# A two-block transformer on one core: the order of steps in the second attention

## The chip, the cores and the metric

The kernel runs on one NeuronCore of a Trainium2 chip. The core has five engines with a queue of instructions each: TensorE (matrix products and transposes, called PE in the profile; its loads of stationary operands are PEld), VectorE (DVE), ScalarE (ACT), GpSimd (POOL) and SyncE (SP), which here issues the transfers. The metric is the device time of one execution in microseconds.

## What is computed

Two transformer blocks on 512 positions of width 1024, in float32. The change touches one part of the second block, the latent attention of its second layer:

```python
def latent_attention(h, pos, w_in, q_norm, kv_norm, w_uq, w_ukv, q_gain, k_gain, w_out):
    c = h @ w_in
    c_q, c_kv, k_rope = jnp.split(c, [Q_LORA, Q_LORA + KV_LORA], axis=-1)      # 256, 128, 32
    q = (rmsnorm_2(c_q, q_norm) @ w_uq).reshape(B, S, B_HEADS, dqk)            # 16 heads, 96
    kv = (rmsnorm_2(c_kv, kv_norm) @ w_ukv).reshape(B, S, B_HEADS, QK_NOPE + V_DIM)
    k_nope, v = jnp.split(kv, [QK_NOPE], axis=-1)                              # 64, 64
    k = jnp.concatenate([k_nope, broadcast k_rope], axis=-1)
    q = rmsnorm_2(q, q_gain); k = rmsnorm_2(k, k_gain)
    # rotary embedding of the last 32 of the 96, causal softmax over 512 keys, then
    # o = p @ v for each head, and o @ w_out
```

Before and behind it stand feed-forward layers (width 2816, three products each), which take most of the time.

## The kernel before

Everything stays on the chip; weights stream in once, as tiles. Products are done in float32 accuracy by splitting each operand in a high part (rounded, written by ScalarE) and a low part (the rest, written by VectorE or GpSimd) and adding three products (lines 1058 to 1060): low by high, high by low, high by high. So nearly every operand costs one ScalarE and one VectorE instruction.

The program is one list of steps, made by `order` and, for this attention, by `attend_b_order`. Each engine walks the same list in order and emits its own part of each step; within an engine nothing is reordered. What links them are semaphores: a step waits for named events of other engines. The order in which steps are listed is therefore the order of work on every engine at once. Buffers go round in rings (`Ring`): `take` gives the next slot and makes its new user wait until the last one has freed it. `banks` are the eight PSUM banks, `tmps` three slots of TMP; `part(k)` cuts a ring off.

The attention runs so. Latents (`b_latent`): c_q in two products (0, 1), c_kv in one (2), k_rope in `b_kr`; ScalarE copies and squares, `b_sumsq` adds the squares with matmuls of one column (line 1295), and `b_factors` turns the sums into the latents' norms on VectorE (lines 2125 to 2145, with a root by three Newton steps). Then the heads come in groups g of two: four units (`b_unit`), u = 2, 3 for keys and values, u = 0, 1 for queries. ScalarE squares a unit (lines 1615, 1623) into the tmps slot and copies it (1619, 1627, 1634), VectorE adds the squares (2154) and makes the values' low part (2162). GpSimd rotates the queries (`b_rotate`, 2298 to 2304), norms both (`b_norm`, 2313 to 2319, the third a power) and scales the keys (`b_scale`, 2329 and 2333).

The head loop then has a software pipeline in it: pass i does the scores of head i (`b_scores`: products at 1333 to 1335, on VectorE the masked maximum at 2186), its exponentials (`b_exp`, 1653), the turning of the next head's queries and keys (`b_qk`: 1069, 1643, 2169), the sum and scaling on GpSimd (`b_sum`: 2200, 2340), the turning of head i - 2 (`b_turns`, three parts of 4, 4 and 2 transposes, line 1343; `b_pt_hi`, 1662; `b_pt_lo`, 2194), and the product with the values of head i - 3 (`b_values`). Passes 0 to 11 also do two units of group i // 2 + 2, and passes from 11 on a part of the output product. Rings in the loop: three banks for scores, two for turned parts, one for the values' sums and two for all else (turned queries and keys, units, output). Two of the three tmps slots are held for exponentials (`third`). ScalarE's split of the weight tiles (1395) and GpSimd's low part (2237) run between these steps.

Of the kernel before, what the change touches and what calls it, by code (L numbers as in the profile page):

```python
# [11 lines left out]
ALU = mybir.AluOpType  # L12
# [4 lines left out]
EPS = 1e-6  # L17
# [720 lines left out]
def attend_b_order(banks, tmps, next_tile, norm_step, hkeys, h_new, h_pair, stats, add_x, do):  # L738
    do("b_begin")

    def latent(i, n):
        banks.take(("b_c", i))
        tmps.take(("t_bc", i))
        do("b_latent", i, n, hkeys())
        norm_step()
# [7 lines left out]
    banks.take(("b_ss",))  # L753
    do("b_sumsq", 1)
    n = next_tile("bq", 0)
# [3 lines left out]
    latent(1, n)  # L759
    do("used", n)  # L760
    do("b_sumsq", 0)
    do("b_factors")

    third = tmps.part(2)
    for n in (3, 2):
        third.take(("t_e", n))
    scored, turned, summed = banks.part(3), banks.part(2), banks.part(1)
    tile = {}

    def unit(g, u):  # L770
        if (u, g % 2) == (2, 0):
            tile[g // 2] = next_tile("bg", g // 2, 1)
# [9 lines left out]
    def head_qk(h):  # L782
        for name in ("b_qt", "b_kt"):
            banks.take((name, h))
        do("b_qk", h)
# [17 lines left out]
    for g in range(2):  # L803
        for u in (2, 3, 0, 1):
            unit(g, u)
        rotate(g)
        do("b_norm", g)
        do("b_scale", g)
    head_qk(0)
    LT, LV, LO = 2, 3, 11  # L810
    for i in range(16 + LV):
        t = i - LT
# [6 lines left out]
        if i < 16:  # L819
            for part in range(3):  # L820
                scored.take(("b_s", i, part))
                do("b_scores", i, part)
            do("b_exp", i, 0)
            if i < 15:
                head_qk(i + 1)
        if i >= LV:
            v = i - LV
            if v % 2 == 0:
                summed.take(("b_o", v // 2))
            do("b_values", v)  # L830
        if i < 16:
            do("b_exp", i, 1)
        if 0 <= t < 16:
            do("b_pt_lo", t, 0)
            do("b_pt_lo", t, 1)
        if i < 16:
            do("b_sum", i)
# [4 lines left out]
        if 0 <= t < 16:  # L842
            turned.take(("b_t", t, 2))
            do("b_turns", t, 2)
            do("b_pt_hi", t, 2)
            do("b_pt_lo", t, 2)
        if i >= LV and (i - LV) % 2:
            attended((i - LV) // 2)
        if i < 12 and i % 2:
            rotate(g)  # L850
            do("b_norm", g)
# [19 lines left out]
def build(nc, a, out, ctx):  # L871
# [182 lines left out]
    def pe_program(pe):  # L1054
# [26 lines left out]
        for kind, *s in steps:  # L1081
# [205 lines left out]
            elif kind == "b_sumsq":  # L1287
                e, = s
                o = vacant(("b_ss",))
# [3 lines left out]
                for n in range(4):  # L1293
                    for i in rows:
                        ins = mm(o[:, 4 * e + n:4 * e + n + 1], tmp(("t_bc", i))[:, 128 * n:128 * n + 128], ones[:, 0:1],
# [20 lines left out]
            elif kind == "b_qk":  # L1316
                h, = s
                x, hl = (h // 2) % 2, h % 2
                pe.wait_ge(*at(("b_rot", h // 2)))
                o = vacant(("b_qt", h))  # L1320
                four(o, lambda n: qts[x][:, n, hl, :], 96).then_inc(*bank_full.up(("b_qt", h)))
                pe.wait_ge(*at(("b_ks", h // 2)))
                o = vacant(("b_kt", h))
                four(o, lambda n: kts[x][:, n, hl, :], 96).then_inc(*bank_full.up(("b_kt", h)))
# [49 lines left out]
    def act_program(act):  # L1374
# [11 lines left out]
        for kind, *s in steps:  # L1386
# [210 lines left out]
            elif kind == "b_kr":  # L1597
                t = vacant(("t_kr",))
                act.wait_ge(*at(("b_kr",)))
                run(t[0:32, :], bank(("b_kr",))[0:32, :], ACT.Copy).then_inc(*act_out.up("b_kr_raw", free=("b_kr",)))  # L1600
            elif kind == "b_kr_turn":
# [5 lines left out]
            elif kind == "b_unit":  # L1607
# [13 lines left out]
                else:  # L1621
# [6 lines left out]
                    act.wait_ge(*at("b_lat"))  # L1628
# [7 lines left out]
            elif kind == "b_qk":  # L1636
                h, = s
                for e, (name, g) in enumerate((("b_qt", gq_b), ("b_kt", gk_b))):
                    act.wait_ge(*at((name, h)))
                    act.wait_ge(*at("small"))  # L1640
                    if h > 1:
                        act.wait_ge(*at(("b_s", h - 2, 2)))
                    run(QK[h % 2][e][0][0:96, :], bank((name, h))[0:96, :], ACT.Copy, scale=g[0:96, :]).then_inc(
# [835 lines left out]
```

## Time and profile before

| | |
|---|---|
| median of 3 runs | 2815.04 us (2812.4 to 2815.44) |
| profiled execution | 2825.3 us, its span 2824.1 us |
| TensorE busy | 2717.6 us, 96% of the span |
| VectorE, ScalarE, GpSimd busy | 1470.3, 974.7, 313.2 us |
| mean granted TensorE clock | 0.976 |
| the second attention, from its latents to its last head | about 2199 to 2429 us of the span |

The span goes from the first to the last instruction. Times in rows are microseconds from its start, unless marked ns. A row of a timeline gives start, duration, engine, line and operation, and in brackets how long the engine had been idle before and what released it. Matmuls overlap, so the sum of their durations is more than the time that they take. Granted clock 1.00 is 2.4 GHz, 0.50 is 1.2 GHz.

### The profile page before, as it was taken

The numbers are of one execution on the slowest core, as the hardware profiler recorded it, in microseconds if no ns is written. First come the engines' busy times: TensorE is split into PE (matmuls) and PEld (weight loads), VectorE is DVE, ScalarE is ACT, GpSimd is POOL, SyncE is SP. The second block draws the span as 40 slices with busy tenths as digits, with TensorE's granted clock in tenths as the row PEclk, the third lists the DMA queues.
The fourth block names the chain that finished last, engine by engine and source line by source line (L and its number), as shares of the span: only waits on it lengthen the run. The fifth ranks groups of instructions, "written<-read, shape, count | busy, mean of one in ns | idle before, by whom it ended". The sixth has DMA issues, their size and how long they took to land.

```text
span 2824.1 us, 32255 instructions
## 1 busy us (share of the span) xinstructions
PE 2717.6 (96%) x13207; PEld 2278.7 (81%) x13207; DVE 1470.3 (52%) x2347; ACT 974.7 (35%) x1601; POOL 313.2 (11%) x381
## 2 busy tenths in 40 slices
PE   6899999999998999998999999999999888999999
PEld 5788788888786888888878888888888778888887
DVE  4635546665657545556665343544434466544433
ACT  3334333333353212234453222322223466432221
POOL 2000000000021000003340000000000467400000
PEclk9999999999999999998999999999999889999999
DMA  4322233623132287746223333232322100132331
GB/s 137 103 92 75 75 105 128 196 79 109 55 115 75 90 104 90 105 84 120 76 65 105 105 98 96 90 105 91 98 94 84 38 31 31 60 119 90 95 96 64
DMA packets 281195, 258.99 MB, mean 92 GB/s; under 512 B 40517, under 2 KB 276056, under 8 KB 281048
## 3 DMA queue, kind: packets, MB, share of 16 engines
q1 hardware_dynamic: 281047, 256.93, 33.1%
q8 instruction: 104, 1.70, 0.3%
q14 instruction: 44, 0.35, 0.0%
HBM read 242.23 MB, written 14.68 MB: 91 GB/s over the span
## 4 chain that ended last, share of the span: by engine, by line
PE 84%; DVE 9%; ACT 4%; issue 1%; SPq 1%; POOL 1%; DMA 1%; DVEq 0%; ACTq 0%; POOLq 0%
PE bank L1058 27%; PE bank L1059 26%; PE bank L1060 26%; DVE Wl L1730 1%; PE bank L1201 1%; PE bank L1069 1%; ACT Wh L1395 1%; SPq L2421 1%; PE bank L1343 1%; DVE Pl L1718 1%; DVE TMP L1923 1%; DVE TMP L1920 1%; DVE TMP L1799 0%; ACT TMP L1508 0%; DMA RAW<-in_a_w_in 0%
## 5 line engine op out<-in xcount | busy, mean ns | idle before, releaser
L1058 PE MATMUL bank<-Hh,Wl 128*128 128x512 f32 x2144 | 845.9, 395 | 15.1 <-DVE Hl L1746 15.1
L1059 PE MATMUL bank<-Hl,Wh 128*128 128x512 f32 x2144 | 838.7, 391 | 0.0
L1060 PE MATMUL bank<-Hh,Wh 128*128 128x512 f32 x2144 | 838.5, 391 | 0.0
L1395 ACT ACTIVATE Wh<-RAW 128x1024 fp32r<-128x1024 f32 (+2 forms) x454 | 441.0, 1023 | 440.6 <-PE bank L1060 378.3
L1730 DVE TENSOR_TENSOR Wl<-RAW,Wh 128x1024 fp32r<-128x1024 f32 (+2 forms) x420 | 492.7, 1216 | 172.2 <-ACT Wh L1395 171.7
L1058 PEld LDWEIGHTS bank<-Hh,Wl 128*128 128x128 f32 x2144 | 404.7, 189 | 103.9 <-issue 8.2
L1058 PE MATMUL bank<-Ph,Wl 128*128 128x512 f32 x1200 | 474.5, 395 | 13.2 <-DVE Pl L1812 3.5
L1060 PEld LDWEIGHTS bank<-Hh,Wh 128*128 128x128 f32 x2144 | 404.5, 189 | 86.3
L1059 PEld LDWEIGHTS bank<-Hl,Wh 128*128 128x128 f32 x2144 | 404.7, 189 | 84.9 <-issue 1.7
L1059 PE MATMUL bank<-Pl,Wh 128*128 128x512 f32 x1200 | 470.6, 392 | 0.0
L1060 PE MATMUL bank<-Ph,Wh 128*128 128x512 f32 x1200 | 470.4, 392 | 0.0
L1788 DVE TENSOR_TENSOR bank<-bank,M 128x512 f32<-128x512 f32 x220 | 150.4, 696 | 387.1 <-PE bank L1060 382.3
L2244 POOL TENSOR_TENSOR TMP<-TMP 128x512 f32<-128x512 f32 x63 | 85.4, 1356 | 1932.1 <-ACT TMP L1417 1930.6
L1058 PEld LDWEIGHTS bank<-Ph,Wl 128*128 128x128 f32 x1200 | 227.4, 190 | 63.8 <-DVE Pl L1718 4.4
L1060 PEld LDWEIGHTS bank<-Ph,Wh 128*128 128x128 f32 x1200 | 227.4, 190 | 48.4
L1936 DVE SCALAR_TENSOR_TENSOR X<-bank,X 128x512 f32<-128x512 f32 x176 | 120.5, 689 | 278.0 <-PE bank L1060 277.4
L1059 PEld LDWEIGHTS bank<-Pl,Wh 128*128 128x128 f32 x1200 | 227.6, 190 | 46.6 <-issue 0.2
L1457 ACT ACTIVATE Ph<-TMP 128x512 fp32r<-128x512 f32 x110 | 69.6, 632 | 485.4 <-DVE TMP L1915 425.3
L1504 ACT ACTIVATE TMP<-bank 128x512 f32<-128x512 f32 x88 | 52.6, 599 | 258.8 <-DVE bank L1788 258.8
L1718 DVE TENSOR_TENSOR Pl<-TMP,Ph 128x512 fp32r<-128x512 f32 x126 | 87.3, 693 | 88.0 <-ACT Ph L1457 76.9
L1058 PE MATMUL bank<-Wh,Hl 128*128 128x256 f32 x288 | 85.5, 297 | 3.0 <-ACT M L1560 3.0
L1059 PE MATMUL bank<-Wl,Hh 128*128 128x256 f32 x288 | 84.1, 292 | 0.0
(296 smaller groups left out, 2506.4 us busy)
## 6 DMA issues: line engine op xcount, KB each, us to landing
RAW<-in_ffn_wg SPq DMA_DIRECT2D x44, 1024.0 KB, 5.3
RAW<-in_ffn_wu SPq DMA_DIRECT2D x44, 1024.0 KB, 5.3
RAW<-in_ffn_wd SPq DMA_DIRECT2D x32, 1024.0 KB, 5.2
RAW<-in_w_up SPq DMA_DIRECT2D x22, 1024.0 KB, 5.1
RAW<-in_w_in SPq DMA_DIRECT2D x20, 1024.0 KB, 5.1
RAW<-in_ffn_wd SPq DMA_DIRECT2D x16, 768.0 KB, 4.4
bias_scratch<-M SPq DMA_DIRECT2D x16, 512.0 KB, 8.0
RAW<-in_w_down SPq DMA_DIRECT2D x8, 1024.0 KB, 5.9
```

Source lines behind the costliest of these rows:

```text
L1058: mm(o, ll, rh, start=start, stop=False)
L1059: mm(o, lh, rl, start=False, stop=False)
L1060: return mm(o, lh, rh, start=False, stop=stop)
L1069: last = turn(o[0:part, 128 * n:128 * n + 128], src(n), ident[:, :])
L1395: run(Wh[:, n % 3, x:y], RAW[:, n % 2, x:y], ACT.Copy).then_inc(*w_hi.up(("w_hi", n, i)))
L1457: run(Ph[:, q, :], tmp(name) if src == "tmp" else bank(name), ACT.Copy).then_inc(*pair_hi.up(("p_hi", q, ver)))
L1504: run(vacant(t), bank(b), ACT.Silu).then_inc(*act_out.up(("silu", t), free=b))
L1718: tt(Pl[:, q, :], src, f(Ph[:, q, :]), ALU.subtract).then_inc(*pair_lo.up(("p", q, ver), free=free))
L1730: tt(Wl[:, n % 3, x:y], RAW[:, n % 2, x:y], f(Wh[:, n % 3, x:y]), ALU.subtract).then_inc(*w_lo.up(*([("w_lo", n)] if i else [])))
L1788: tt(bank(b), bank(b), RVIEW[norm_R[nv]], ALU.mult).then_inc(*dve_out.up(("scaled", b)))
L1936: stt(X[:, c, :], bank(b), factor, X[:, c, :], ALU.mult, ALU.add).then_inc(*x_new.up(("x", ver, c), free=b))
L2244: tt(SQ, SQ, tmp(("t_sq", nv, c)), ALU.add).then_inc(*pool_out.up(("sq", nv, c), free=("t_sq", nv, c)))
```

## The change

Only the order of steps in the second attention and what they wait for changes; the arithmetic is the same, but for one dummy exponential.

- In the loop, the third part of the turns (T2, its high and its low part) is listed ahead of the product with the values and of the units; the low part of part 0 is listed directly behind the high parts, that of part 1 behind the first exponential. `b_qk` is cut in a query half and a key half.
- In front of the loop, `b_factors` is cut in two. The key latents' half is listed behind their sum, ahead of the first query latent. The units of keys and values of groups 0 and 1, the key half of their norm, and the key scaling of group 0 are listed around the second query latent. Query units, rotations and the query half of the norms follow. The cut of the rings is made only then; the query latents use the two tmps slots of `third` from the start.
- ScalarE does one exponential of one column behind the raw copy of the rotary key, so that its table is loaded there.

```diff
 def attend_b_order(...):
     do("b_begin")
+    third = tmps.part(2)
     def latent(i, n):
         banks.take(("b_c", i))
-        tmps.take(("t_bc", i))
+        (third if i < 2 else tmps).take(("t_bc", i))
...
-    banks.take(("b_ss",))
+    banks.take(("b_ss", 1))
     do("b_sumsq", 1)
+    do("b_factors", 1)
     n = next_tile("bq", 0)
     latent(0, n)
     banks.take(("b_krt",))
     do("b_kr_turn")
-    latent(1, n)
-    do("used", n)
-    do("b_sumsq", 0)
-    do("b_factors")
-
-    third = tmps.part(2)
-    for n in (3, 2):
-        third.take(("t_e", n))
-    scored, turned, summed = banks.part(3), banks.part(2), banks.part(1)
...
-            tile[g // 2] = next_tile("bg", g // 2, 1)
+            tile[g // 2] = next_tile("bg", g // 2, 1 if g else 0)
...
-    def head_qk(h):
-        for name in ("b_qt", "b_kt"):
-            banks.take((name, h))
-        do("b_qk", h)
+    def head_qk(h, e):
+        banks.take((("b_qt", "b_kt")[e], h))
+        do("b_qk", h, e)
...
-    for g in range(2):
-        for u in (2, 3, 0, 1):
-            unit(g, u)
-        rotate(g)
-        do("b_norm", g)
-        do("b_scale", g)
-    head_qk(0)
+    for u in (2, 3):
+        unit(0, u)
+    do("b_norm", 0, 8, 16)
+    do("b_scale", 0)
+    latent(1, n)
+    do("used", n)
+    for u in (2, 3):
+        unit(1, u)
+    do("b_norm", 1, 8, 16)
+    banks.take(("b_ss", 0))
+    do("b_sumsq", 0)
+    do("b_factors", 0)
+    for u in (0, 1):
+        unit(0, u)
+    rotate(0)
+    do("b_norm", 0, 0, 8)
+    head_qk(0, 1)
+    for u in (0, 1):
+        unit(1, u)
+    head_qk(0, 0)
+    do("b_scale", 1)
+    rotate(1)
+    do("b_norm", 1, 0, 8)
+    for n in (3, 2):
+        third.take(("t_e", n))
+    scored, turned, summed = banks.part(3), banks.part(2), banks.part(1)
     LT, LV, LO = 2, 3, 11
     for i in range(16 + LV):
-        t = i - LT
+        t, v = i - LT, i - LV
         if 0 <= t < 16:
             for part in range(2):
                 turned.take(("b_t", t, part))
                 do("b_turns", t, part)
             do("b_pt_hi", t, 0)
             do("b_pt_hi", t, 1)
-        if i < 16:
-            for part in range(3):
-                scored.take(("b_s", i, part))
-                do("b_scores", i, part)
-            do("b_exp", i, 0)
-            if i < 15:
-                head_qk(i + 1)
-        if i >= LV:
-            v = i - LV
+            do("b_pt_lo", t, 0)
+        for part in range(3) if i < 16 else ():
+            scored.take(("b_s", i, part))
+            do("b_scores", i, part)
+            if part == 0:
+                do("b_exp", i, 0)
+                if 0 <= t:
+                    do("b_pt_lo", t, 1)
+        if t in (14, 15):
+            do("b_pt_lo", t, 1)
+        if i < 15:
+            for e in range(2):
+                head_qk(i + 1, e)
+        if 0 <= t < 16:
+            turned.take(("b_t", t, 2))
+            do("b_turns", t, 2)
+            do("b_pt_hi", t, 2)
+            do("b_pt_lo", t, 2)
+        if v >= 0:
             if v % 2 == 0:
                 summed.take(("b_o", v // 2))
             do("b_values", v)
         if i < 16:
             do("b_exp", i, 1)
-        if 0 <= t < 16:
-            do("b_pt_lo", t, 0)
-            do("b_pt_lo", t, 1)
-        if i < 16:
             do("b_sum", i)
         if i < 12:
             g = i // 2 + 2
             for u in (0, 1) if i % 2 else (2, 3):
                 unit(g, u)
-        if 0 <= t < 16:
-            turned.take(("b_t", t, 2))
-            do("b_turns", t, 2)
-            do("b_pt_hi", t, 2)
-            do("b_pt_lo", t, 2)
...
@@ ScalarE, b_kr
                 run(t[0:32, :], bank(("b_kr",))[0:32, :], ACT.Copy).then_inc(*act_out.up("b_kr_raw", free=("b_kr",)))
+                run(sm[:, 13:14], mhalf, ACT.Exp)
@@ ScalarE, b_unit
-                    act.wait_ge(*at("b_lat"))
+                    act.wait_ge(*at(("b_lat", 1)))
@@ VectorE, b_factors: the same operations on 4 columns of one half, the root for each half
+                e, = s
+                cols, both = slice(4 * e, 4 * e + 4), slice(8 * e, 8 * e + 8)
...
@@ GpSimd, b_norm on columns c0 to c1 (8 to 16 keys, 0 to 8 queries)
-                g, = s
+                g, c0, c1 = s
...
+                if c1 == 16:
+                    pool.wait_ge(*at(("b_factors", 1)))
+                    pool.wait_ge(*at("b_shift_k"))
+                    pool.wait_ge(*at(("b_uss", g, 3)))
+                if c0 == 0:
+                    pool.wait_ge(*at(("b_factors", 0)))
+                    pool.wait_ge(*at(("b_uss", g, 1)))
...
+                tt(y, v, mhalf.broadcast_to([128, c1 - c0]), ALU.pow).then_inc(*pool_out.up(("b_y", g, c0)))
```

## Rows read from the trace of the kernel before

**Rows 1.** Windows: stretch, its us, busy us of each engine (count), clock, DMA.
```profile
2224.15:2249.37 25.22, 16.04 (x97) 14.71 (x97) 11.28 (x41) 11.52 (x29) 10.09 (x17) 0.75 0.00 1
2249.37:2269.45 20.08, 17.71 (x77) 16.39 (x78) 10.20 (x29) 11.66 (x33) 13.56 (x16) 0.58 0.17 54
2269.45:2379.89 110.44, 93.07 (x603) 86.39 (x602) 71.65 (x185) 76.10 (x202) 74.74 (x103) 0.88 0.05 20
2323.39:2343.98 20.59, 16.14 (x120) 15.12 (x120) 14.30 (x38) 15.89 (x42) 14.25 (x21) 0.97 0.00 1
2379.89:2407.70 27.81, 26.25 (x165) 23.34 (x163) 19.52 (x47) 15.95 (x42) 18.45 (x22) 1.00 0.11 39
```

**Rows 2.** Waits of TensorE, 2190 to 2440: for whom, us in total, times, longest.
```profile
PE bank L1343 <- DVE Pl L2194: 17.8, 12, 3.3
PE bank L1058 <- DVE Hl L2169: 3.5, 3, 1.7
```

**Rows 3.** Windows with TensorE alone, first and last half-clock stretch.
```profile
2226.70:2236.90 10.20, 8.09 (x38) 0.50 0.00 1
2366.60:2373.40 6.80, 6.80 (x27) 0.50 0.00 0
```

**Rows 4.** Timeline of one change of passes, on ScalarE, VectorE and TensorE.
```profile
2354.68 0.49 ACT L1615 ACTIVATE TMP<-bank 128x384 f32<-128x384 f32 x1 [0.53 <-PE bank L1060]
...
2355.20 0.55 DVE L2154 TENSOR_REDUCE pkf<-TMP 128x4 f32<-128x384 f32 x1 [0.85 <-ACT TMP L1615]
...
2355.43 0.88 ACT L1662 ACTIVATE Ph<-bank 128x256 fp32r<-128x256 f32 x2
...
2355.86 0.42 DVE L2194 TENSOR_TENSOR Pl<-bank,Ph 128x256 fp32r<-128x256 f32 x1
...
2356.34 0.33 PE L1343 MATMUL bank<-ident,M 128*128 128x128 f32 x1 [1.10 <-DVE Pl L2194]
```

**Rows 5.** Instructions on Ph, 2262 to 2430: ns min/median/max, starts, forms.
```profile
L1662 ACT ACTIVATE Ph<-bank x48: 383/597/674, 2270.3 to 2424.2; 128x512 fp32r<-128x512 f32 x32, 128x256 fp32r<-128x256 f32 x16
L2194 DVE TENSOR_TENSOR Pl<-bank,Ph x48: 415/677/692, 2275.6 to 2424.6; 128x512 fp32r<-128x512 f32 x32, 128x256 fp32r<-128x256 f32 x16
```

**Rows 6.** Timeline: one head's first maximum (VectorE) and first exponential (ScalarE).
```profile
2357.83 0.81 DVE L2186 CUSTOM_DVE_ANT_0 M<-bank,maskb,sm 128x512 f32<-128x512 f32 x1 [1.55 <-PE bank L1335]
...
2358.68 0.72 ACT L1653 ACTIVATE M<-M,pkf 128x512 f32<-128x512 f32 x1 [1.06 <-DVE pkf L2186]
```

**Rows 7.** Timeline of TensorE, the waits of the opening.
```profile
2225.50 2.51 PE L1295 MATMUL bank<-ones,TMP 128*128 128x1 f32 x16 [1.36 <-ACT TMP L1596]
...
2232.89 0.53 PE L1058 MATMUL bank<-Wh,Pl 128*128 128x192 f32 x1 [2.11 <-DVE Pl L2162]
...
2246.85 0.87 PE L1069 MATMUL bank<-ident,M 128*96 128x128 f32 x4 [2.70 <-POOL M L2333]
2249.37 0.77 PE L1333 MATMUL bank<-Hh,Hl 96*128 96x512 f32 x1 [1.65 <-DVE Hl L2169]
```

**Rows 8.** Timeline of ScalarE: the table load and the first exponential.
```profile
2248.46 1.28 ACT L1653 ACT_TABLE_LOAD   x1
2251.99 0.72 ACT L1653 ACTIVATE Z<-Z,pkf 128x512 f32<-128x512 f32 x1 [2.25 <-DVE pkf L2186]
```

**Rows 9.** Timeline of GpSimd: rotation and norm of group 0.
```profile
2238.82 0.74 POOL L2298 TENSOR_TENSOR pki<-M,ropt 128x256 f32<-128x256 f32 x1 [22.68 <-ACT M L1619]
...
2241.29 0.22 POOL L2313 TENSOR_TENSOR pkf<-pkf 128x16 f32<-128x16 f32 x1
...
2241.89 2.91 POOL L2317 TENSOR_TENSOR pkf<-pkf,sm 128x16 f32<-128x16 f32 x1
```

**Rows 10.** Timeline of VectorE: a latent's low part, first and last factor step.
```profile
2219.43 0.75 DVE L2101 SCALAR_TENSOR_TENSOR Pl<-bank,P,Ph 128x512 fp32r<-128x512 f32 x1 [8.92 <-ACT TMP L1596]
...
2228.50 0.17 DVE L2129 TENSOR_TENSOR pkf<-bank,pkf 128x8 f32<-128x8 f32 x1 [2.21 <-PE bank L1295]
...
2231.83 0.17 DVE L2145 COPY pkf<-pkf 128x8 f32<-128x8 f32 x1
```

## What I expect of the change

> Names used below. A pass is one round of the head loop, i = 0 to 18. In it T0, T1, T2 are the turns (transposes) of parts 0, 1, 2 of head t = i - 2; H and L are ScalarE's high copy and VectorE's low part of one of them. S0 to S2 are the scores of head i, M0 to M2 VectorE's masked maxima of them, E0 and E1 ScalarE's exponentials of part 0 and of parts 1 and 2. QT and KT turn the next head's queries and keys, QH, KH, QL, KL are their high and low parts. V is the product with the values (head i - 3), U the two units of the projections (keys and values in even passes, queries in odd ones).
>
> **What bounds the kernel now.** I read first where TensorE isn't the limit. The stretches on both sides of the second attention are full of its matmuls at full clock; from about 2224 to 2430 us they aren't. The windows view [rows 1] shows three kinds of loss: the opening (2224.15 to the first scores at 2249.37) has TensorE busy 16.04 of 25.22 us; passes 0 and 1 have it busy 17.71 of 20.08, but at a mean clock of 0.58; passes 2 to 11 have it busy 93.07 of 110.44 at 0.88; and in passes 12 to 14 only 1.56 of 27.81 us are idle. The waits view [rows 2] names the largest wait: 17.8 us in 12 waits of a turn (line 1343) for the low part of an earlier turn. The windows of the granted clock [rows 3] give the second loss: TensorE is at 0.50 of full speed (1.2 instead of 2.4 GHz) in seven stretches between 2226.7 and 2373.4, of which the first and the last are shown; each begins soon after a wait of 1.3 us or more, and none after one of the four waits of 1.10 us.
>
> Why the turn waits is in the order of one pass change [rows 4]. The turned ring has two banks, so T1 of the next head needs the bank of T2, and T2 comes last in the pass. ScalarE squares and copies the last unit, then takes H2 (the first of the pair at 2355.43); VectorE reduces the square, then takes L2 (2355.86); TensorE starts T1 at 2356.34, 1.10 us after it ran dry. After units of keys and values the same chain has four more copies in front, and the wait is 1.9 to 3.3 us. So in the loop TensorE waits for a drain of both other engines once in every pass, while each of them is busy less than three quarters of the time: in passes 2 to 11 ScalarE 76.10, VectorE 71.65, GpSimd 74.74 of 110.44 us [rows 1].
>
> **The loop, passes 2 to 11.** T2, H2 and L2 now stand ahead of V and U. T2 needs the bank of T0, which L0 gives back; L0 is now issued directly behind H0 and H1, some 1.3 us after ScalarE takes H0 (0.60 + 0.68 by the medians of [rows 5]), and T2 comes only behind three scores and eight turns, more than 3 us later. H2 and L2 then run under V and U, and the wait of 1.1 to 3.3 us per pass goes. What is late next? On TensorE, 93.07 us at a mean clock of 0.88 is 81.9 us at full clock, the floor. ScalarE has 76.10 us of work and gets a new wait: E0 needs M0, M0 needs L0 and S0, and L0 needs H0. From the start of H0 that is 0.60 + 0.68 + 0.81 [rows 5, 6] and a tenth for the handoff, 2.2 us, of which H0 and H1 fill 1.2: 1.0 us idle in each pass, 86.1 us for ten. GpSimd (74.74) and VectorE (71.65) are under both. The two limits alternate: passes with keys and values have the shorter TensorE work and the longer ScalarE work, those with queries the reverse, and the ring of two banks (QT, KT, U) doesn't let one run a pass ahead. For this I add 0.35 us a pass, an estimate between nothing and the 0.9 us by which the unit work of the two kinds differs: 89.6 us. With one half-clock stretch of 6.8 us instead of about four (half of it lost, 3.3): 92.9 us. The loop gives 110.44 - 92.9 = **17.5 us**. The ends: the floor of 81.9 and some tenths per pass, 26 us; and, if waits of 1 us a pass come back at other places, 10.5 us.
>
> **The opening.** Key factors and scaling move under the query latents. All of it is off the path by rows: VectorE is idle 8.92 us before its latent part at 2219.43 [rows 10], and the second root costs some 13 small operations of 0.17 us and a step of 0.2 us each, 2.6 us. What remains on the path, step by step: the last latent product ended before 2224.15 and now ends one pair of key units later; a second pair and the 16 sums follow. At the full clock a pair is about 1.45 us and the sums 1.9 (2.51 at half clock in [rows 7]), which puts their end at 2224.15 + 1.45 + 1.45 + 1.9 = 2228.95. The query factors take 3.5 us (2228.50 to 2231.83 and the last 0.17 [rows 10]): 2232.45. The units of queries have one TMP slot between them, since the other two now belong to the latents and later to the exponentials, so the second square waits for the first's reduction: 0.55, then 0.49 and about as much again for the copy [rows 4], 2234.0. The rotation on GpSimd takes 2.47 us (2238.82 to 2241.29 [rows 9]): 2236.5. From a turn to the first scores it is 2.52 us now (2246.85 to 2249.37 [rows 7]): 2239.0. TensorE itself would be there at 2237.8 or so (16.04 us, of which 8.09 at half clock shrink to 4, plus the last wait of 1.65), so the chain over the query factors, rotation and turn sets it. The opening gives 2249.37 - 2239.0 = **10.4 us**; 6 if the clock falls again in it, 12 if the chain overlaps better. Of the waits in [rows 7], the 1.36 is covered by units, the 2.11 goes because the eight banks aren't yet split when the key units run, the 2.70 is the norm with its power of 2.91 us and the scaling [rows 9], which for keys lies early now.
>
> The halves of the norm: four power operations on 8 columns for two on 16. One on 8 costs between nearly nothing (0.22, the multiplication on 16) and 2.91 us [rows 9]; I take 2.91, as a power is unlike a multiplication. Only the query half of group 0 is near the path (M0 of head 0 needs it): 0 to 0.5 us, taken as 0.
>
> **The early exp table: nothing.** The load takes 1.28 us at 2248.46, but ScalarE then still waits 2.25 us for M0 before the first exponential at 2251.99 [rows 8]. A load ended there anyway; it would cost up to 1.28 us only if M0 came earlier. At its new place ScalarE idles for the query latents. The Trainium skill (ScalarE: Activation LUTs, What ACT_TABLE_LOAD costs) gives 1283 ns for every load, and the trace has just that; reckoned by that alone the edit would give 1.3 us more, the row says it gives none. Neutral too: one tile fewer asked ahead for group 0 (its split was already issued with the tile before), and the new wait of the raw key copy for the sums. No DMA changes its place in its queue.
>
> **Passes 0 and 1.** Their TensorE work is 17.71 x 0.58 = 10.3 us at full clock. The opening still ends in two waits (for the rotation, for QL) of the size after which the clock fell, so I take a mean clock of 0.75, 13.7 us, and keep the 2.4 us of waits that stand there now: 16.1 for 20.08, **4.0 us**, between 0 and 9.
>
> **Passes 12 to 17.** Passes 12 to 15 lose their waits of half a microsecond, 1.6 us in all [rows 1]. Passes 16 and 17 get worse: there are no scores left between T0 and T2, and V stood between them before. T2 now waits for H0 and L0, 0.60 + 0.68 and three handoffs, less T1's four turns of some 0.45: 1.15 us each, **2.3 us lost**.
>
> **Sum:** 17.5 + 10.4 + 4.0 + 1.6 - 2.3 = 31.2 us. The profiled execution has a span of 2824.1 us and would have 2792.9. It took 2825.3 in all, 0.4% over the median of 2815.04 of the runs shown; I take the gain as the same there: 2783.8 us.
>
> **Rivals.** (a) The wait moves instead of going: U needs QL's bank, QT the bank of U, and with ScalarE at some 86 of 93 us each late copy shows. GpSimd makes it likelier: 14.25 us in a pair of passes of 20.59 [rows 1], in a fixed order in which the keys of group g stand behind two scalings and a weight split. Two passes then take 20.0 us instead of 18.6, and more half-clock stretches stay: the loop gives 10.5, the opening 8, passes 0 and 1 2.5, with the rest 20.3 in all, 2794.7 us. (b) The clock stays low by what TensorE does, not by its waits: turns and narrow products go on as before, and the stretches of [rows 3] with them. Then the loop keeps its clock loss of some 11 us where I kept 3.3, and passes 0 and 1 keep theirs: 31.2 - 7.7 - 4 = 19.5, 2795 us. For it speaks that [rows 3] has TensorE busy 6.80 of 6.80 us at half clock; against it, that each stretch began behind a long wait. [...] (c) TensorE's floor is reached nearly everywhere: 42 us, 2773. (d) Slower: T2 in front of V makes ScalarE's lag into TensorE's. If H0 starts more than about 2.3 us behind T0, T2 stops, and V and U behind it, which delays ScalarE's next units in turn. To end 0.2% slower it must cost 37 us, 2.6 us in each of 14 passes, with H0 some 5 us late: 2821 us. ScalarE's 76.10 us of work in 110.44 speak against. (e) The waits come back whole, as the loop is held by the chain M0, E0, QH, QL: 2815 within 5.
>
> **Chances.** Forecast (2776 to 2790) 0.47, (a) 0.20, (b) 0.12, (c) 0.12, (d) 0.04, (e) 0.05. About 0.2%, 5.6 us, is what a measurement of this kernel can tell from no change: faster 0.91, same 0.05, slower 0.04. The range goes from 2771 (44 us: most of (c)) to 2802 (13 us: the lower ends of the loop, 10.5, and of the opening, 6, with nothing from passes 0 and 1).
>
> **What would show it.** Right: no wait of line 1343 for line 2194 in passes 3 to 11, short waits at the first unit or at QT in their place; ScalarE with about 1 us in front of E0 in each pass; first scores near 2239; one wait of about 1.15 us at T2 in each of the last two passes with turns; half-clock stretches in the opening and pass 0 alone, or one more. Wrong: half-clock stretches behind no wait (b), QT or KT waiting for GpSimd or for a unit's bank (a), T2 waiting for L0 in the middle of the loop (d).

## The result and the profile after

The changed kernel takes 2788.74 us (median of 4 runs, 2787.54 to 2790.39); the kernel before took 2815.24 beside it. The ratio is 0.9904, 95% interval 0.9887 to 0.9922: 26.5 us faster. A second set on another chip gave 2789.21 against 2816.31 and again 0.9904 (0.9890 to 0.9918).

The windows view of the kernel after, with the columns of [rows 1] and cut at the same places, but for the first stretch, which starts at the turn of the rotary key (then passes 0 and 1, passes 2 to 11, passes 12 to 14):

```profile
2214.07:2235.25 21.18, 17.30 (x125) 15.80 (x125) 13.20 (x47) 12.17 (x34) 11.13 (x20) 0.98 0.09 32
2235.25:2253.98 18.73, 15.60 (x77) 14.19 (x78) 10.20 (x29) 11.31 (x32) 14.55 (x22) 0.68 0.17 58
2253.98:2344.75 90.77, 82.57 (x601) 77.22 (x601) 70.22 (x185) 74.04 (x202) 74.78 (x103) 1.00 0.07 24
2344.75:2370.36 25.61, 25.61 (x164) 23.22 (x162) 19.21 (x47) 15.58 (x42) 18.11 (x23) 1.00 0.14 43
```

The first of these stretches in the kernel before:

```profile
2218.04:2249.37 31.33, 22.14 (x126) 19.46 (x125) 13.38 (x48) 13.41 (x35) 10.09 (x17) 0.80 0.05 19
```

Passes 2 to 11 went from 110.44 to 90.77 us. The work of the other three engines in them is what it was to within a few us; TensorE does the same products in 82.57 us instead of 93.07, since its clock is at full speed nearly throughout (1.00 for 0.88), and its idle time fell from 17.4 to 8.2 us. What is left of idle time has changed its cause. Waits of TensorE, 2190 to 2440, kernel after:

```profile
PE bank L1070 <- DVE Hl L2183: 9.1, 8, 2.3
PE bank L1353 <- DVE Pl L2208: 2.9, 4, 1.0
PE bank L1081 <- POOL M L2318: 2.2, 1, 2.2
PE bank L1343 <- DVE Hl L2183: 1.6, 1, 1.6
PE bank L1081 <- DVE Pl L2176: 0.9, 3, 0.4
```

Line 1353 is the turn and 2208 the low part, 1343 and 2194 before: 2.9 us stand where [rows 2] has 17.8. The waits of the first matmul of a unit (1070) for the low part of the turned queries (2183) have grown from 3.5 to 9.1 us. The clock, with TensorE alone, in the two half-clock stretches that are left of the seven behind [rows 3]:

```profile
2234.30:2244.50 10.20, 8.54 (x33) 0.50 0.00 0
2251.40:2254.80 3.40, 3.40 (x18) 0.50 0.64 245
```

The first begins within the second of the two waits at the end of the opening (1.65 us, over at 2235.25), the second 1.4 us behind a wait of 2.28 us in pass 1. This is one trace. In a second one of the same kernel, a half-clock stretch begins where TensorE waited for nothing, in the opening:

```profile
2214.80:2227.00 12.20, 12.20 (x82) 1.00 0.15 55
2227.00:2230.40 3.40, 3.40 (x18) 0.50 0.00 0
```

So a long wait isn't the only thing that the low clock follows here; the section on the prediction comes back to this.

### The profile page after: what moved, and what is told of

The parts are those of the page before. It is cut to its first block, busy times and chain, and to the rows that moved or that the text cites. A ratio compares the mean times of both kernels' runs of the same rounds, so it can differ in the third digit from the quotient of the medians.

```text
span 2789.2 us, 32273 instructions
## 1 busy us (share of the span) xinstructions
PE 2696.5 (97%) x13207; PEld 2260.6 (81%) x13207; DVE 1473.3 (53%) x2362; ACT 972.5 (35%) x1602; POOL 315.3 (11%) x389
## 4 chain that ended last, share of the span: by engine, by line
PE 86%; DVE 8%; ACT 4%; issue 1%; POOL 0%; SPq 0%; DMA 0%; DVEq 0%; ACTq 0%; POOLq 0%
PE bank L1070 28%; PE bank L1072 27%; PE bank L1071 27%; DVE Wl L1741 1%; PE bank L1213 1%; PE bank L1081 1%; ACT Wh L1405 1%; DVE TMP L1934 1%; DVE TMP L1931 1%; DVE TMP L1810 1%; ACT TMP L1518 0%; DVE Pl L1729 0%; ACT Hh L1418 0%; PE bank L1264 0%; DVE nt L1714 0%
```

## The experiments

All of them are whole kernels, and all but the first are edits of the changed kernel. Times by stretch come from each kernel's trace: from the turn of the rotary key to the first scores; from the scores of head 0 to those of head 2, from 2 to 12, from 12 to 15; and from the scores of head 15 to the last product with the values. The sixth column sums the half-clock stretches of the attention in the trace's clock records, to about 0.2 us.

| kernel | opening | 0 to 2 | 2 to 12 | 12 to 15 | rest | half clock | median us (before beside it) |
|---|---|---|---|---|---|---|---|
| before | 31.33 | 21.44 | 109.71 | 27.79 | 18.45 | 54.5 | 2815.24 |
| changed | 21.18 | 19.92 | 90.37 | 25.61 | 20.75 | 13.6 | 2788.74 (2815.24) |
| changed, again | 21.21 | 18.97 | 90.97 | 25.60 | 20.76 | 13.6 | 2789.21 (2816.31) |
| loop only | 31.12 | 19.69 | 90.69 | 25.61 | 20.76 | 20.4 | 2799.44 (2817.42) |
| opening only | 21.19 | 18.88 | 106.85 | 27.77 | 18.42 | 27.2 | 2805.32 (2817.42) |
| no early exp | 21.20 | 18.94 | 90.36 | 25.61 | 20.76 | 10.2 | 2789.16 (2817.42) |
| late low parts | 21.19 | 18.90 | 121.08 | 35.01 | 24.22 | 44.2 | 2832.29 (2817.42) |
| early low parts only | 21.21 | 18.96 | 107.83 | 25.56 | 18.33 | 30.6 | 2802.55 (2816.31) |
| repaired tail | 21.22 | 18.97 | 90.94 | 25.61 | 18.33 | 13.6 | 2785.27 (2819.80) |
| factors behind units | 23.71 | 19.90 | 90.67 | 25.59 | 20.75 | 13.6 | 2792.84 (2819.80) |
| heads turned early | 21.22 | 18.91 | 96.79 | 25.63 | 20.78 | 23.8 | 2793.73 (2819.80) |
| three edits | 23.68 | 19.92 | 95.12 | 25.63 | 18.35 | 23.8 | 2795.18 (2819.80) |
| low part 1 behind heads | 21.21 | 18.85 | 87.91 | 25.59 | 18.33 | 13.6 | 2784.05 (2816.31) |
| exp behind heads | 21.18 | 20.46 | 91.59 | 25.61 | 18.33 | 13.6 | 2787.48 (2816.31) |

The same code at the same stretch repeats in traces to about a tenth in the opening, from 12 to 15 and in the rest, to 0.6 us from 2 to 12, and to 1 us from 0 to 2, where the clock falls. The unchanged code ahead of the attention doesn't repeat so well: in the traces of the edited kernels its end, the turn of the rotary key, lies between 2209.2 and 2215.5 us. Kernels that were measured together, with the same median of before, are compared first. The medians of before differ by up to 4.6 us between the sets, so a few us between edited kernels of different sets are read from the stretches; neither medians nor ratios can tell them.

### Which half gives what

The kernel before with the loop of the changed one, and the changed kernel with the old loop:

```diff
 # loop only: the kernel before, with the new body of the pass loop
-            for e in range(2):
-                head_qk(i + 1, e)
+            head_qk(i + 1)
 # opening only: the changed kernel, with the old body of the pass loop
-                head_qk(i + 1)
+                for e in range(2):
+                    head_qk(i + 1, e)
```

> The kernel before with the new order of the head loop alone; the opening is untouched. If the loop's order carries its own gain (waits of the turns gone, and with them half-clock stretches), passes 2 to 11 take 90 to 93 us instead of 110.4, the tail loses 2.5, and the kernel is 16 to 20 us faster than before. If the clock's part came from the opening or from chance (the profiled execution of before was slower than its median), it is only 12 to 14 us faster, with half-clock stretches left in the loop.

> The changed kernel with the old order of the head loop. If opening and loop add up, the first scores start 10 us earlier behind the turn of the rotary key than before, the kernel is 8 to 11 us faster than before, and the loop shows the waits of a turn for a low part again, 14 to 18 us in sum. If instead the loop was held by what the opening delays, the loop gets shorter too and the gain is over 13 us.

Loop only: ratio 0.9936 (0.9923 to 0.9950), 18.0 us by medians. Opening only: 0.9958 (0.9945 to 0.9971), 12.1 us, a little over the 8 to 11 expected. Together 30.1, where the kernel without the early exponential, which is as fast as the changed one and was measured with these two, had 28.3: they add up within what the medians can tell. In the table each half has the changed kernel's length in its own stretches and about that of before in the others, but for passes 0 and 1, which are shorter in both (19.69 and 18.88 for 21.44); the loop isn't shorter for the opening. With the old loop the windows view has, for passes 2 to 11 counted from the scores of head 2:

```profile
2253.89:2360.74 106.85, 89.52 (x603) 83.27 (x602) 71.98 (x186) 75.56 (x202) 75.36 (x105) 0.92 0.06 20
```

and its waits of a turn for a low part are again 17.8 us in 12, as in [rows 2]. But the mean clock is 0.92, where the traced execution of before had 0.88: the same order lost less to the clock this time, 27.2 us of half-clock stretches in the attention instead of 54.5.

### The early exponential

```diff
-                run(sm[:, 13:14], mhalf, ACT.Exp)
```

> The changed kernel without the dummy exponential. If the table load is covered at its old place, the time is that of the changed kernel within 0.5 us (0.9904 of before), with the load of 1.28 us ahead of the first exponential inside ScalarE's wait. If a load counts wherever it stands, it is 1.3 us slower than the changed kernel.

2789.16 us, ratio 0.9903 (0.9888 to 0.9918), the same span in the trace (2789.2) as the changed kernel. The load is worth nothing at either place, as read from [rows 8].

### Both halves of the loop's order

The low parts of parts 0 and 1 go back behind those of the turned heads; part 2 stays ahead of the values:

```diff
             do("b_pt_hi", t, 1)
-            do("b_pt_lo", t, 0)
...
-                if 0 <= t:
-                    do("b_pt_lo", t, 1)
...
             do("b_turns", t, 2)
+            do("b_pt_lo", t, 0)
+            do("b_pt_lo", t, 1)
             do("b_pt_hi", t, 2)
```

> The changed kernel, with the third part of the turns still ahead of the values, but the low parts of parts 0 and 1 behind the turned keys as before. If the early low parts are what lets the third part stand ahead of the values, the turn of part 2 now waits for the low part of part 0 in every pass, about 2 to 3 us, and the kernel is 15 to 30 us slower than the changed one, near or over the time of before. If the place of part 2 alone matters, it stays within 3 us of the changed kernel.

2832.29 us, ratio 1.0054 (1.0036 to 1.0071): slower than the kernel before, and 43.1 us slower than the kernel without the early exponential that was measured with it, more than the 15 to 30 expected. This is rival (d) with its wait brought about. The waits view of TensorE, then one pass on VectorE and TensorE (in this kernel 1350 is the turn, 2180 the low parts of the turned heads, 2205 that of a turned part):

```profile
PE bank L1350 <- DVE Pl L2205: 39.4, 16, 4.1
```

```profile
2303.27 1.40 DVE L2180 SCALAR_TENSOR_TENSOR Hl<-bank,sm,Hh 96x512 fp32r<-96x512 f32 x2
2304.60 1.27 DVE L2205 TENSOR_TENSOR Pl<-bank,Ph 128x512 fp32r<-128x512 f32 x2
...
2305.33 0.33 PE L1350 MATMUL bank<-ident,Z 128*128 128x128 f32 x1 [2.39 <-DVE Pl L2205]
```

T2 stands 2.39 us for L0, which VectorE takes up only at 2304.60, behind four maxima and two low parts; the products with the values, whose data are there, stand behind it. Sixteen such waits cost more than the change gains.

The other half alone: early low parts, but part 2 behind values and units.

```diff
-        if 0 <= t < 16:
-            turned.take(("b_t", t, 2))
-            do("b_turns", t, 2)
-            do("b_pt_hi", t, 2)
-            do("b_pt_lo", t, 2)
         if v >= 0:
             ...
             do("b_values", v)
         ...                        # exponentials, sum, units
+        if 0 <= t < 16:
+            turned.take(("b_t", t, 2))
+            do("b_turns", t, 2)
+            do("b_pt_hi", t, 2)
+            do("b_pt_lo", t, 2)
```

> The changed kernel with the early low parts of parts 0 and 1, but the turn of part 2 again behind the values and the units. If both halves of the loop's new order are needed, the waits of a turn for the low part of part 2 are back, 14 to 18 us in sum, and it is 14 to 20 us slower than the changed kernel. If the early low parts carry the gain, it stays within 4 us of it.

2802.55 us, 13.3 slower than the changed kernel measured with it (14 to 20 were expected), 0.9954 (0.9940 to 0.9968) of before. The waits of a turn are back:

```profile
PE bank L1353 <- DVE Pl L2208: 15.3, 9, 3.3
```

So the loop's gain (18.0 us by the medians of the loop-only kernel) needs both: the place of T2 removes the wait, the early L0 makes the place possible. The early low parts alone give nothing from head 2 to 12 (107.83 us, where the kernel with neither half has 106.85); they only clear the half microsecond of passes 12 to 15 (25.56 against 27.79) and leave the tail unharmed (18.33).

### The tail

```diff
-        if 0 <= t < 16:
+        if 0 <= t < 14:
             (turn, high and low part of part 2)
         if v >= 0:
             ...
             do("b_values", v)
+        if t in (14, 15):
+            (turn, high and low part of part 2)
```

> The changed kernel with the product with the values ahead of part 2 again, in passes 16 and 17 alone. If the two waits of 0.98 us there are the cost of the new order, both go and the kernel is 2 us faster than the changed one (2.5 if the passes shrink to their old length). If the time comes back at the next product, nothing changes.

2785.27 us, ratio 0.9881 (0.9867 to 0.9895). In the trace the rest behind the scores of head 15 takes 18.33 us for 20.75, the length that it had before, 2.4 less. What goes are these waits of the changed kernel, timeline of TensorE in passes 16 and 17:

```profile
2380.02 0.44 PE L1353 MATMUL bank<-ident,TMP 128*128 128x128 f32 x2 [0.98 <-DVE Pl L2208]
...
2386.97 0.44 PE L1353 MATMUL bank<-ident,Z 128*128 128x128 f32 x2 [0.98 <-DVE Pl L2208]
```

### The opening

```diff
-    do("b_factors", 0)
     for u in (0, 1):
         unit(0, u)
+    do("b_factors", 0)
     rotate(0)
```

> The changed kernel with the query factors listed behind the two query units of group 0, so that VectorE reduces their squares first. If the chain over factors, the single TMP slot, the copy and the rotation sets the first scores, TensorE's wait of 2.23 us for the rotation goes and the first scores come 2 us earlier; the kernel is 1 to 2.5 us faster than the changed one. If the first maximum waits for the query norm instead, the gain is taken back at it and the kernel is the same.

2792.84 us, ratio 0.9906 (0.9891 to 0.9920), neither the gain nor the same time: in the trace the opening is 2.5 us longer (23.71 for 21.18). The wait for the rotation is gone, but another of 4.68 us stands ahead of the first scores. VectorE works in the order of the list, and the low parts of the turned keys and queries are now behind the factors. The chain moved from one place of the list to another and did not get shorter; it even grew. The first and the last of the factor steps, in the changed kernel and then with the edit, with one of the steps that took longer:

```profile
2225.76 0.15 DVE L2146 TENSOR_TENSOR pkf<-bank,pkf 128x4 f32<-128x4 f32 x1
...
2228.80 0.16 DVE L2158 TENSOR_SCALAR pkf<-pkf 128x8 f32<-128x8 f32 x1
```

```profile
2231.30 0.15 DVE L2146 TENSOR_TENSOR pkf<-bank,pkf 128x4 f32<-128x4 f32 x1
...
2231.48 0.51 DVE L2149 TENSOR_SCALAR nt<-pkf 128x4 f32<-128x4 f32 x1
...
2235.49 0.16 DVE L2158 TENSOR_SCALAR pkf<-pkf 128x8 f32<-128x8 f32 x1
...
2239.16 0.77 PE L1343 MATMUL bank<-Hh,Hl 96*128 96x512 f32 x1 [4.68 <-DVE Hl L2183]
```

The same chain takes 4.4 us instead of 3.2: in it, five steps take 0.32 to 0.51 us while GpSimd rotates beside them (2231.24 to 2233.78), and 0.16 or 0.17 behind that (below).

### What holds the new loop

The timeline of the changed kernel shows the wait of a query pass. ScalarE takes the first exponential after 1.15 us of waiting, then QH and KH (1654); VectorE comes to QL (2183) only at 2285.13, behind L1 (2208) and three maxima (2200); TensorE then starts the unit at 2285.93:

```profile
2283.25 0.72 ACT L1664 ACTIVATE TMP<-TMP,pkf 128x512 f32<-128x512 f32 x1 [1.15 <-DVE pkf L2200]
...
2283.98 1.24 ACT L1654 ACTIVATE Hh<-bank,sm 96x512 fp32r<-96x512 f32 x2
...
2283.14 0.69 DVE L2208 TENSOR_TENSOR Pl<-bank,Ph 128x512 fp32r<-128x512 f32 x1
...
2285.13 1.40 DVE L2183 SCALAR_TENSOR_TENSOR Hl<-bank,sm,Hh 96x512 fp32r<-96x512 f32 x2
...
2285.93 0.35 PE L1070 MATMUL bank<-Wh,Pl 128*128 128x192 f32 x1 [1.07 <-DVE Hl L2183]
```

Three edits were made against it. The first turns the heads ahead of the second and third part of the scores:

```diff
             do("b_scores", i, part)
             if part == 0:
+                if i < 15:
+                    for e in range(2):
+                        head_qk(i + 1, e)
                 do("b_exp", i, 0)
...
-        if i < 15:
-            for e in range(2):
-                head_qk(i + 1, e)
```

> The changed kernel with the next head's queries and keys turned behind the first part of the scores, ahead of parts 1 and 2, and copied ahead of the first exponential. If the loop is now held by ScalarE's wait for the first maximum and the late low part of the turned queries (waits of the units, 9.1 us in all), the copies fill ScalarE's wait, the units' waits go and the kernel is 5 to 9 us faster. If the banks of the last units are the limit, the turns wait for them instead and the kernel is the same or up to 5 us slower.

2793.73 us, ratio 0.9910 (0.9897 to 0.9923); the stretch from head 2 to 12 is 96.79 us for 90.4. The banks are the limit, the second of the two cases. The turns of the heads now come before the last units of keys and values have given their banks back:

```profile
PE bank L1081 <- DVE Pl L2176: 9.5, 11, 2.8
```

The second puts ScalarE's first exponential behind QH and KH (with the repaired tail):

```diff
             do("b_scores", i, part)
-            if part == 0:
-                do("b_exp", i, 0)
...
             for e in range(2):
                 head_qk(i + 1, e)
+        if i < 16:
+            do("b_exp", i, 0)
```

> The changed kernel with the repaired tail, and the first exponential behind ScalarE's copies of the turned heads. If ScalarE's wait of 1 us for the first maximum in each pass is what costs, the copies fill it, QL comes earlier, and it is 2 to 5 us faster than the repaired tail alone. If the turned heads come later than the first maximum does, ScalarE waits for them instead and it is the same or up to 5 us slower.

2787.48 us, ratio 0.9899 (0.9885 to 0.9914), no better than the repaired tail; 91.59 us from head 2 to 12, and the units wait 9.5 us, with 1.07 to 1.08 in each of the last four query passes as in the changed kernel. ScalarE's wait ahead of E0 is gone in all passes but the last, and the time isn't shorter. So it was no cost of its own: VectorE still reaches QL behind the maxima.

The third leaves ScalarE alone and moves L1 on VectorE behind the low parts of the heads (with the repaired tail):

```diff
             if part == 0:
                 do("b_exp", i, 0)
-                if 0 <= t:
-                    do("b_pt_lo", t, 1)
-        if t in (14, 15):
-            do("b_pt_lo", t, 1)
         if i < 15:
             for e in range(2):
                 head_qk(i + 1, e)
+        if 0 <= t < 16:
+            do("b_pt_lo", t, 1)
```

> The changed kernel with the repaired tail, and the low part of part 1 behind the low parts of the turned heads instead of ahead of the second maximum. If what holds the query passes is VectorE's order (QL comes 0.7 us late behind that low part), the waits of the units fall from 1.07 to about 0.4 us each and it is 2 to 4 us faster than the repaired tail alone (0.9881). If ScalarE's wait for the first maximum holds the pass, the wait moves and the time stays within 1 us.

2784.05 us, ratio 0.9887 (0.9872 to 0.9903), against 2789.21 for the changed kernel measured with it (0.9904, 0.9890 to 0.9918): 5.2 us by medians, though the intervals overlap. Against the repaired tail alone, which the expectation named, no gain is shown (2784.05 for 2785.27 us, but 0.9887 for 0.9881); the two weren't measured together. The traces have 2.4 us against the changed kernel in the tail, which is the repaired tail's, and 3.1 from head 2 to 12 (87.91 for 90.97, and for 90.94 with the repaired tail); 2.5 of them against the trace of the changed kernel whose clock was full there (90.37). The wait of the same query pass went from 1.07 to 0.62, that of the other three late query passes to 0.60 to 0.62, where 0.4 was expected:

```profile
2282.50 1.40 DVE L2186 SCALAR_TENSOR_TENSOR Hl<-bank,sm,Hh 96x512 fp32r<-96x512 f32 x2
...
2283.30 0.36 PE L1073 MATMUL bank<-Wh,Pl 128*128 128x192 f32 x1 [0.62 <-DVE Hl L2186]
```

So the query passes are held by VectorE's order ahead of QL, not by ScalarE's wait. That the whole kernel is faster than with the repaired tail alone is not shown.

The repaired tail, the query factors behind the units and the heads turned early were also put together:

> All three edits at once. If they act at different places their gains add up: 8 to 13 us faster than the changed kernel. If one covers another it is less than the best of them plus 1 us.

2795.18 us, 0.9917 (0.9904 to 0.9930), slower than the changed kernel, which neither case allowed for: each of the three keeps its own effect in its own stretch (23.68, 95.12, 18.35), and two of them are losses.

### The changed kernel again

> The changed kernel itself, on the chip of the next three, so that small differences are read against it. It should again be at about 0.9904 of before. If the shortfall against the trace (the attention is 30.9 us shorter there, the medians 26.5) came from the sample of before, the gain by medians moves to between 27 and 31 us here.

27.1 us by medians, where the first set had 26.5: at the lower edge of the range for that, so the sample of before explains little of the 4 us between medians and traces. The attention takes 177.5 us in this trace and 177.8 in the first.

## Why the prediction was right, and where its sizes were off

The time, 2788.7 us, is inside the range and in the band of the likeliest case (2776 to 2790), 4.9 us above the predicted 2783.8. In the traces the whole attention, from the turn of the rotary key to the last product with the values, went from 208.7 to 177.8 us: 30.9 us, where the sum said 31.2. That this comes to 0.3 us is luck: the terms have errors of both signs, and the trace of before seems to have lost more than usual (the step that missed, below).

- **The loop.** Predicted 92.9 us for passes 2 to 11, measured 90.77. Mechanism right: the waits of the turns fell from 17.8 to 2.9 us (two of 0.49 us in these passes, two of 0.98 in the tail), and what came in their place was what rival (a) names, units waiting for QL, about 1.07 us in each of the last four query passes. I had put that at 0.35 us a pass on top of ScalarE's 86.1: 89.6, or about 0.8 us of idle TensorE a pass, as measured, but for the wrong reason. ScalarE's wait of 1 us ahead of E0 isn't new: [rows 6] has one of 1.06 in the kernel before, where it is 0.96 to 1.54 us in each of passes 2 to 11, as it is 0.99 to 1.15 now. And giving ScalarE other work in it moved nothing, while VectorE's order did. The clock term was too careful: I kept one stretch of 6.8 us, the trace has less than 1 us of one, and the second trace one of 3.4.
- **The clock, rival (b).** It fell for the loop. With the same matmuls the mean clock of passes 2 to 11 is 1.00 for 0.88 [rows 1]. From head 2 to 12, the eight traces with the new loop (the third edit against QL among them) have no half-clock stretch in six and one of 3.4 us in two; the four in which a turn of a part waits for its bank have 17 to 27 us, and the two with the heads turned early 7 and 10. But that a long wait brings the low clock, as I read it from [rows 3], is neither needed nor enough. In ten of the twelve traces with the new opening, and so in the rows above (2227.00), a half-clock stretch of 3.4 us begins with no wait ahead of it; 16 products of one column, the sums of squares, stand 1.3 us before it, and in the first trace of the same kernel the clock stayed full behind the same 16. And of the waits of the kernel before, that of 1.93 us at 2323.39 was followed by no low clock. The long waits that do have one behind them are for VectorE mostly, and for GpSimd (2.70 in [rows 7]) and ScalarE (1.36), in no place for a DMA. So the waits and the low clock went together, and what ends the full clock stays open. The Trainium skill (TensorE: Matmul & The Clock Gate, Loop structure matters more than you think) shows a loop in which VectorE copies the result out of PSUM while the next matmuls follow at once, and says that such a copy doesn't take TensorE out of its warm state. The changed loop is that case, and agrees; the section doesn't speak of matmuls that wait for the copy.
- **The opening.** Predicted 10.4 us, measured 10.15 (21.18 for 31.33). The chain was the predicted one: a wait of 2.23 us for the rotation, then 1.65 for QL. That it sets the first scores and TensorE doesn't, eight other traces with this opening confirm: a half-clock stretch lies in it, TensorE is busy for 18.93 us of it instead of 17.30, the wait for the rotation shrinks to 0.6, and the opening takes 21.2 us all the same. What I took as 0, the query half of the norm, is 0: the first maximum starts 1.77 us behind the first scores, 1.76 in the kernel before.
- **Passes 0 and 1.** Predicted 4.0 us, measured 1.4 (18.73 for 20.08). The term was mis-sized: I took a mean clock of 0.75 and it was 0.68, with one stretch of 10.2 us begun in the opening's last wait, and the wait for QL in pass 1 grew from 1.67 to 2.28 us. Part of it is the draw: in the second trace of the same kernel the mean clock is 0.82 from the scores of head 0 to those of head 2, and these take 18.97 us for 19.92.
- **Passes 12 to 17.** The gain in 12 to 14 is 2.2 us for the 1.6 that I had for 12 to 15: with T2 in front no half microsecond is left, and TensorE is busy 25.61 of 25.61 us. The loss in the tail is 2.3 us (20.75 for 18.45), as predicted, though each wait is 0.98 and not 1.15. The repaired tail shows that it was avoidable.
- **The step that missed** is the last one: "I take the gain as the same there". The profiled execution of before was 10 us over its median, that of after 1.7 over its own. 4.0 us of the difference between the two traces lie ahead of the attention (its rotary key is turned at 2218.04 and 2214.07), where nothing was changed and the edited kernels differ among themselves by up to 6 us. The rest lies in it, as far as can be told: if loop and opening add up, as their medians do, the traces of the two half changes (187.9 and 193.1 us) and of the changed kernel (177.5) put the usual attention of before at 187.9 + 193.1 - 177.5 = 203.5 us, 5.2 less than traced, and the gain at 26.0, which is what the medians show. That the clock is the reason is likely but not shown: the trace of before had 54.5 us of half-clock stretches, the one with the same loop and the new opening 27.2. I should have taken the clock's part at less than one trace showed.
- **The early exponential**: nothing, as predicted from [rows 8] (2789.16 us without it).

Open stays why the kernel before spreads by 10 us between runs (2811.7 to 2821.5), when the changed one spreads by 3 to 8.

## What to carry to other kernels

When the last step of a pass gives back the buffer that the first step of the next pass needs, move it ahead of long work that needs neither, and check on the engine that frees the buffer that its own step is moved forward too: with the new opening in all three, the early low parts alone ended 14 us faster than before (0.9954, most of it the opening's), the early turn alone 15 us slower (1.0054), and both together 27 us faster. Where such an order rests on work that hides the chain, treat the passes in which that work is absent by themselves. And where one trace has much of its loss in the clock, read it as one draw: compare its total with the median before the clock's part goes into a sum, and look at a second trace of the same kernel before a rule for the clock is read from the first.

## What the runs showed of the hardware

The power on GpSimd isn't priced like its other operations: on 128x8 it takes 1.65 us, on 128x16 2.91 [rows 9], by these two about 0.16 us per column and 0.4 fixed (an estimate), where a multiplication takes 0.20 and 0.22. So halving its columns saves 43% of it; the prediction took 2.91 for the half too.

Small VectorE operations can take several times their 0.17 us while GpSimd works. In the changed kernel two steps of the key factors, VectorE, and the weight split beside them, GpSimd:

```profile
2211.47 1.55 DVE L2155 TENSOR_TENSOR pkf<-pkf 128x4 f32<-128x4 f32 x1
2213.05 1.49 DVE L2157 TENSOR_SCALAR pkf<-pkf 128x8 f32<-128x8 f32 x1
...
2211.43 3.09 POOL L2251 TENSOR_TENSOR Wl<-RAW,Wh 128x640 fp32r<-128x640 f32 x2 [6.83 <-ACT Wh L1405]
```

Each of the two ends with one of the two halves of the split. The Trainium skill (SBUF — State Buffer, SBUF: two separate sides) says that VectorE and GpSimd share one pair of ports, which one of them holds for a whole instruction while the other is blocked; of VectorE's instructions it names those with two inputs in SBUF and those in a mode that uses both ports. The rows of the split agree. Here it was hidden, as VectorE had time; in the experiment on the query factors, beside the rotation, it is nearly all of the 1.2 us by which the chain grew.

Not every GpSimd instruction does this. Beside the power, VectorE's steps of the query factors keep their length in the changed kernel, the same lines that took 0.38 and 0.39 us beside the rotation:

```profile
2225.49 1.64 POOL L2336 TENSOR_TENSOR pkf<-pkf,sm 128x8 f32<-128x8 f32 x1
...
2226.15 0.17 DVE L1708 TENSOR_SCALAR nt<-nt 128x4 int32<-128x4 int32 x1
...
2226.96 0.16 DVE L1718 SCALAR_TENSOR_TENSOR pkf<-nt,pkf 128x4 f32<-128x4 f32 x1
```

The second of them has two inputs in SBUF, so by the section the power would block it until 2227.13, and the measurement shows that it doesn't. Why the two cases differ, no run here shows.
